# A two-block model kernel on one core: setup by halves of the features, first projections pulled into it, bias rows moved behind the turning of the tokens

## The reference

```python
mod_x = silu(c) @ w_mod + b_mod            # shift | scale | gate, 1024 each; the same for c_ctx
hx = rmsnorm(x, norm_g) * (1 + sc_x) + sh_x          # 512 tokens
hc = rmsnorm(ctx, norm_g) * (1 + sc_c) + sh_c        # 256 tokens
z  = h @ w_in        # aq, ak, av, ag, alr, bq, bk, bv, bg, bbeta, bdec, mg
alog = log_sigmoid(alr @ gla_up + gla_ub) / 16       # decay of the first mixer, both directions
# a gated linear attention over chunks of 64 (aq, ak, av, alog) and a gated delta rule
# (bq, bk, bv), both forward and backward; gated, merged, projected by w_o, gated, added to x
```

## Time and profile before

| | |
|---|---|
| median of 3 runs | 1430.29 us (1427.27 to 1430.88) |
| the profiled execution's own time | 1430.24 us |
| its span, first to last instruction | 1428.1 us |
| TensorE busy | 1360.0 us (95% of the span) |
| VectorE / ScalarE / GpSimd busy | 623.8 / 412.3 / 330.2 us |
| TensorE's share of the chain that ended last | 87% |
| mean granted TensorE clock | 0.987 |

### The profile page before, as it was taken

The page is one execution under the profiler, slowest core; times in us unless marked ns, Lnnn a source line. Parts: engine busy times, 40 slices in busy tenths (PEclk is TensorE's granted clock), DMA queues, the critical chain, the costliest instruction groups (busy, mean ns, idle before and its releaser), DMA issues.

```text
span 1428.1 us, 22760 instructions
## 1 busy us (share of the span) xinstructions
PE 1360.0 (95%) x9123; PEld 775.6 (54%) x9123; DVE 623.8 (44%) x1330; ACT 412.3 (29%) x892; POOL 330.2 (23%) x422
## 2 busy tenths in 40 slices
PE   4999989999999999999999999998899999999897
PEld 2454645555566777764444655445554645445553
DVE  3364264975234333452146321226745330326735
ACT  3332031226332222110002301235732211226631
POOL 0200000112123443210043000025733000016731
PEclk9999989999999999999999999999999999999999
DMA  9611000211230010003241612311000713210001
GB/s 335 213 59 55 5 33 27 74 59 40 79 120 3 3 61 3 3 1 132 104 152 51 159 55 59 148 59 49 1 16 1 185 51 107 81 57 1 2 1 59
DMA packets 71512, 96.48 MB, mean 68 GB/s; under 512 B 27623, under 2 KB 35231, under 8 KB 71406
## 3 DMA queue, kind: packets, MB, share of 16 engines
q1 hardware_dynamic: 71034, 94.76, 19.8%
q10 hardware_dynamic: 372, 0.27, 0.1%
HBM read 92.89 MB, written 2.13 MB: 67 GB/s over the span
## 4 chain that ended last, share of the span: by engine, by line
PE 87%; DVE 7%; ACT 2%; issue 2%; POOL 1%; DMA 1%; ACTq 0%; DVEq 0%; POOLq 0%
PE PS L147 83%; PE PS L2543 2%; DVE AR L2649 1%; ACT AR L2771 1%; DVE AR L2636 1%; DMA AR<-in_onehot 1%; DVE AR L1900 0%; POOL AR L2849 0%; PE PS L347 0%; DVE AR L812 0%; POOL AR L2830 0%; PE PS L1958 0%; ACT AR L2781 0%; DVE AR L773 0%; POOL AR L370 0%
## 5 line engine op out<-in xcount | busy, mean ns | idle before, releaser
L147 PE MATMUL PS<-AR 64*64 64x64 f32 (+13 forms) x8534 | 1291.6, 347 | 28.3 <-ACT AR L2781 6.6
L147 PEld LDWEIGHTS PS<-AR 64*64 64x64 f32 (+4 forms) x8534 | 711.3, 156 | 580.0 <-issue 487.3
L2771 ACT ACTIVATE AR<-AR 128x257 f32<-128x257 f32 (+5 forms) x160 | 84.9, 530 | 104.9 <-DVE AR L2649 96.0
L370 POOL TENSOR_TENSOR AR<-AR 128x1 f32<-128x1 f32 (+4 forms) x26 | 21.9, 840 | 359.9 <-DVE AR L365 313.2
L2649 DVE CUSTOM_DVE_ANT_0 AR<-PS,AR 128x257 f32<-128x257 f32 (+5 forms) x160 | 72.3, 452 | 67.3 <-PE PS L147 49.3
L1107 DVE SCALAR_TENSOR_TENSOR AR<-AR 128x441 f32<-128x441 f32 (+2 forms) x96 | 78.5, 818 | 17.9 <-ACT AR L1064 14.3
L1493 DVE TENSOR_TENSOR AR<-PS,AR 128x256 f32<-128x256 f32 x60 | 25.5, 425 | 114.6 <-PE PS L147 111.5
L2830 POOL TENSOR_SCALAR AR<-AR 128x257 f32<-128x257 f32 (+5 forms) x96 | 53.4, 557 | 62.6 <-DVE AR L2655 55.0
L1847 POOL TENSOR_TENSOR AR<-AR 128x512 f32<-128x512 f32 x36 | 47.5, 1319 | 58.9 <-DMA AR<-in_w_o 55.8
L2543 PE MATMUL PS<-AR 128*128 128x128 f32 x352 | 51.2, 283 | 8.4 <-DVE AR L2636 6.3
L1620 ACT ACTIVATE AR<-PS 128x512 f32<-128x512 f32 x48 | 28.7, 597 | 101.8 <-PE PS L147 99.4
(11 more groups left out here) (253 smaller groups left out, 823.5 us busy)
## 6 DMA issues: line engine op xcount, KB each, us to landing
AR<-in_w_in SPq DMA_DIRECT2D x17, 2048.0 KB, 8.9
AR<-in_w_mod SPq DMA_DIRECT2D x6, 2048.0 KB, 16.4
AR<-in_w_out SPq DMA_DIRECT2D x4, 2048.0 KB, 12.8
AR<-in_x SPq DMA_DIRECT2D x8, 512.0 KB, 5.5
AR<-in_w_o SPq DMA_DIRECT2D x2, 2048.0 KB, 8.5
AR<-in_w_in SPq DMA_DIRECT2D x2, 1664.0 KB, 8.8
AR<-in_w_in SPq DMA_DIRECT2D x12, 256.0 KB, 4.1
AR<-in_w_gla_out SPq DMA_DIRECT2D x1, 2048.0 KB, 8.9
```

The lines of the kernel that those rows point to most:

```text
L147: return t.matmul(o, l, r, start=s, stop=p, skip_group_check=True)
L2771: a_.do.activation(P, P, ACT.Exp, bias=mn[:, j % NJS, e:e + 1], scale=-1.0, accum_out=su[:, j % NJS, e:e + 1]).then_inc(sa, na("p", l, j, e))
```

## The change

1. SP issues `w_mod` parts 0 and 2 (shift and scale of features 0 to 511), load 0 and the first four feature tiles of load 1 (semaphore `s_aq`), then `w_mod` parts 1 and 3 and the last four tiles of load 1. One transfer more than before; the same bytes.
2. TensorE's bias row matmuls stand behind `mod_turned(2)`, VectorE's copies of them behind the modulation of the first half.
3. Modulation goes by halves: k = 0, 2 and tiles 0 to 3 of `hT` and `hC`, then k = 1, 3 and tiles 4 to 7. VectorE's `turned` is split in `row` (copy) and `turned`.
4. Halves of the first projections stand between these steps: `low_rank(t, 0)`, `queries(0, 0, 4)`, `queries(1, 0, 2)`, `queries(1, 2, 4)`. Their second halves and the rest stand in `gla_t`.
5. Several accumulators get named banks, and `ps.ring` is set to seven banks for `u` and `bb`.
6. In `gla_t` the second half of the `aq` 1 projection stands before `key(0)`, where it stood behind it. `gla_v`, `gla_a` and `gla_g` are unchanged.

The diff, cut to what matters (the removed loops are described above):

```diff
@@ setup_s
-        for k in range(4):
-            s.go.dma_start(wmod[:, k], wm(512 * k)[0]).then_inc(s_wm[k], 16)
-        load(s, 0)
-        load(s, 1)
+        aq, = wviews(1)
+        for half, ks in ((0, (0, 2)), (1, (1, 3))):
+            for k in ks:
+                s.go.dma_start(wmod[:, k], wm(512 * k)[0]).then_inc(s_wm[k], 16)
+            if half == 0:
+                load(s, 0)
+            sl = slice(4 * half, 4 * half + 4)
+            s.go.dma_start(aq[:, sl, :], wl[1][0][0][:, sl, :]).then_inc(s_ring[ring_slot(1)] if half else s_aq, 16)
@@ setup_t
-            p = ps.take(t, "mod", k)
+            p = ps.take(t, "mod", k, bank=k // 2 if k % 2 else None)
-            p = ps.take(t, "modT", k)
+            p = ps.take(t, "modT", k, bank=2 + k // 2 if k % 2 else None)
...
+        mod(2)
         mod_turned(0)
-        for k in range(1, 4):
-            mod(k)
-            mod_turned(k)
+        mod_turned(2)
+        t.wait_ge(s_oh, 32)
+        t.wait_ge(sv, nv["rt"])
+        for i, (k, lo, hi) in enumerate(BIAS):
+            p = ps.take(t, "brow", k, lo, bank=i)
+            mm(t.go, p[0:13, 0:hi - lo], rt[0:33, 0:13], oh[0:33, 640 * k + lo:640 * k + hi], True, True).then_inc(st, nt("brow", k, lo))
+        low_rank(t, 0)
+        mod(1)
+        queries(t, 0, 0, 4)
+        mod_turned(1)
+        mod(3)
+        queries(t, 1, 0, 2)
+        mod_turned(3)
+        queries(t, 1, 2, 4)
+    def low_rank(t, half):
...
+            b = 4 if lo else 5
+            p = ps.banks[b] if half else ps.take(t, "alr", lo, bank=b)
+            for i in range(2 * half, 2 * half + 2):
...
+    def queries(t, a, t0, t1):
+        w, = weights(t, 1) if t0 >= 4 else wviews(1)
+        t.wait_ge(s_aq, 16)
+        p = ps.banks[6 + a] if t0 else ps.take(t, "aq", a, bank=6 + a)
+        for t8 in range(t0, t1):
...
+        if t1 == 8:
+            x.then_inc(st, nt("aq", a))
@@ setup_v
+        row(0)
         for m in range(0, 8, 2):
             v.wait_ge(st, nt["hC", m])
...
+        row(2)
+        turned(0)
+        turned(2)
+        modulated(0)
+        for k, lo, hi in BIAS:
+            v.wait_ge(st, nt["brow", k, lo])
...
+        row(1)
+        turned(1)
+        row(3)
+        turned(3)
+        modulated(1)
@@ setup_a
+        for half in range(2):
+            for k in (half, 2 + half):
+                a.wait_ge(sv, nv["modAB", k])
...
@@ gla_t
+        low_rank(t, 1)
+        queries(t, 0, 4, 8)
+        ps.ring = list(range(7))
...
-        query(0)
         t.wait_ge(s_up, 64)
         t.wait_ge(sv, nv["alr", 0])
         for q, lo, hi in UQ:
...
         x.then_inc(st, nt("bb"))
+        queries(t, 1, 4, 8)
+        ps.ring = list(range(8))
         key(0)
-        query(1)
         key(1)
```

More of the change, by code:

```diff
@@ L287, in program @@
     s_wm = [landing(f"w_mod{k}") for k in range(4)]
+    s_aq = landing("gla_queries_first_half")
     s_x = [landing(f"x{i}") for i in range(6)]
@@ L356, in setup_t @@
             x.then_inc(st, nt("hC", m))
+        mod(2)
         mod_turned(0)
-        for k in range(1, 4):
-            mod(k)
-            mod_turned(k)
-        nt.mark("at", "setup")
+        mod_turned(2)
[12 more added lines that the diff above has]
+        queries(t, 1, 2, 4)
+        nt.mark("at", "setup")
+    def low_rank(t, half):
+        w, = weights(t, 0)
+        for lo, hi in XC:
+            hx, h = (hT, "hT") if lo else (hC, "hC")
+            b = 4 if lo else 5
+            p = ps.banks[b] if half else ps.take(t, "alr", lo, bank=b)
+            for i in range(2 * half, 2 * half + 2):
+                for q in range(2):
+                    t8 = 2 * i + q
+                    t.wait_ge(*((sa, na[h, t8]) if t8 % 2 else (sv, nv[h, t8])))
+                    x = mm(t.go, p[64 * q:64 * q + 64, 0:hi - lo], w[:, t8, :], hx[:, t8, :], i == 0, i == 3)
+            if half:
+                x.then_inc(st, nt("alr", lo))
+        if half:
+            nt.mark("weights", 0)
+    def queries(t, a, t0, t1):
[3 more added lines that the diff above has]
+        for t8 in range(t0, t1):
+            t.wait_ge(*((sa, na["hT", t8]) if t8 % 2 else (sv, nv["hT", t8])))
+            x = mm(t.go, p[:, :], w[:, t8, 128 * a:128 * a + 128], hT[:, t8, :], t8 == 0, t8 == 7)
+        if t1 == 8:
+            x.then_inc(st, nt("aq", a))
     def rsq_v(v, o, x, scale, *name):
@@ L387, in setup_v, with row @@
         v.do.scalar_tensor_tensor(out=bg, in0=vc("bmod", 8, 8), scalar=1.0, in1=vc("norm_g", 0, 8), op0=ALU.add, op1=ALU.mult).then_inc(sv, nv())
[L388 to L393, removed]
+        def row(k):
             v.wait_ge(st, nt["mod", k])
@@ L397, in turned @@
             ps.empty(sv, nv, "mod", k)
+        def turned(k):
             c = slice(4 * (k % 2), 4 * (k % 2) + 4)
@@ L408, in turned, with modulated @@
             ps.empty(sv, nv, "modT", k)
+        def modulated(half):
+            for m in range(4 * half, 4 * half + 4, 2):
+                v.do.tensor_scalar(hT[:, m, :], hT[:, m, :], modA[:, m:m + 1], modB[:, m:m + 1], ALU.mult, ALU.add).then_inc(sv, nv("hT", m))
+            for m in range(4 * half, 4 * half + 4, 2):
+                v.do.tensor_scalar(hC[:, m, :], hC[:, m, :], modA[:, 8 + m:9 + m], modB[:, 8 + m:9 + m], ALU.mult, ALU.add).then_inc(sv, nv("hC", m))
         v.wait_ge(sa, na["squares", 5])
@@ L425, in setup_v @@
             ps.empty(sv, nv, "hC", m)
[L426 to L432, removed]
+        row(2)
[4 more added lines that the diff above has]
+            v.wait_ge(st, nt["brow", k, lo])
+            v.do.tensor_copy(brow[0:13, 640 * k + lo:640 * k + hi], ps["brow", k, lo][0:13, 0:hi - lo]).then_inc(sv, nv("brow"))
+            ps.empty(sv, nv, "brow", k, lo)
+        row(1)
[3 more added lines that the diff above has]
+        modulated(1)
         nv.mark("at", "setup")
@@ L455, in setup_a @@
             ps.empty(sa, na, "hC", m)
[L456 to L461, removed]
+        for half in range(2):
+            for k in (half, 2 + half):
+                a.wait_ge(sv, nv["modAB", k])
+            for m in range(4 * half + 1, 4 * half + 4, 2):
+                a.do.activation(hT[:, m, :], hT[:, m, :], ACT.Identity, bias=modB[:, m:m + 1], scale=modA[:, m:m + 1]).then_inc(sa, na("hT", m))
+            for m in range(4 * half + 1, 4 * half + 4, 2):
+                a.do.activation(hC[:, m, :], hC[:, m, :], ACT.Identity, bias=modB[:, 8 + m:9 + m], scale=modA[:, 8 + m:9 + m]).then_inc(sa, na("hC", m))
         na.mark("at", "setup")
@@ L554, in gla_t @@
     def gla_t(t):
[L555 to L565, removed]
+        low_rank(t, 1)
+        queries(t, 0, 4, 8)
+        ps.ring = list(range(7))
         w, = weights(t, 1)
-        def query(a):
-            p = ps.take(t, "aq", a)
-            projT(t, p, w, 128 * a, 128, 256, 768, ("aq", a))
         def key(a):
```

5 lines of the change are left out of this document (removed).

## The result

| | before | after |
|---|---|---|
| median, 4 runs each (lowest to highest) | 1430.05 us (1427.27 to 1430.88) | 1439.57 us (1437.88 to 1444.14) |
| ratio, 95% interval | | 1.0071 (1.005 to 1.0092) |
| profiled execution, its span | 1430.24, 1428.1 us | 1437.88, 1435.7 us |

The change makes the kernel slower by about 0.7%, clear of the 0.3% that a measurement can tell; the forecast was 1440.2 us. The profiled execution after is the fastest of its four, so its trace says +7.6 us where the medians say +9.5.

A forecast was written before the change was run, and what follows sets the result against it. TensorE (87% of the chain) bounds the kernel, but VectorE's chain decides until the second turning. Stall +7.3, cold clock +1.5 and +1.5, banks -0.3 make +10.0 on 1430.24: 1440.2 us, range 1435.5 to 1443.5.

The forecast's parts named there:

- The deciding mechanism: First mixer: key(0) waits 10.5 us for ScalarE's late copy of aq 1; queries and second turning move +7.3 us before clock.
- the count of banks: First mixer's ring: key(0) takes k = 31, bank 7, the bank of aq 1; before, k = 42, bank 2.
- the wait for `key(1)` that goes: VectorE's copies in the first mixer: its 1.61 us wait for key(1) disappears, so +8.9 becomes +7.3 us.
- What the setup gains (c): TensorE's setup steps: aq 0 done about 52.8 instead of 58.3, 5.5 us ahead, plus 3.4 us of aq 1 done.
- That most of the lead can't be spent (d): Before u: TensorE idles 2.8 us for up, held by bias rows landing at 52; u starts 2.5 us earlier.
- the rivals on the landing of the bias rows: Setup transfers: earlier landing gives 1437.3 us (chance 0.05); later setup or transfers give 1442 to 1444 us (0.10).
- the rule on the order of completions: Transfer queues: completions are not first in, first out per issuing engine, so bias row stores may land earlier: -2.9 us.
- The sum: Whole kernel: +7.3 + 1.5 + 1.5 - 0.3 = +10.0 us on 1430.24, so 1440.2 us.
- 1.5 of clock: key(0) starts cold after 10.5 us of idle TensorE, making VectorE's sums 1.5 us later.
- the gap of about 3 us ending at 55.7: Sign in TensorE's timeline: idle for about 3 us before u, ended at 55.7 by the transfer of up.
- the one on the other side (no stall): First mixer: key(0) gets a bank other than 7, the gain stands, 1426 to 1428 us; chance 0.05.
- The one in which the change doesn't do what it says: Setup: turning doesn't start earlier, the 5.6 us lead is gone, u starts near 58: +2.5, 1442.7 us.

The follow-up runs named there:

- experiment 1: Changed kernel with the ring kept at seven banks until key(1) is issued, so key(0) avoids the bank of aq 1: 1427.18 us, ratio 0.9991.
- experiment 3: Kernel before, with only query(1) put ahead of key(0) and key(0) taking the bank of aq 1: 1446.51 us, ratio 1.0111.
- experiment 6: Changed kernel, seam fixed (ring cut, key(0) first), up loaded during setup, u behind alr, second aq halves behind key(0), aq copies after the logarithm: 1427.7 us, ratio 0.9975.
- experiment 2: Changed kernel with the ring at seven banks until key(1) and key(0) back ahead of the second half of aq 1: 1426.2 us, ratio 0.9981.
- experiment 5: Changed kernel with seven-bank ring and key(0) ahead of aq 1's second half, bias rows moved back ahead of the turning: 1431.84 us, ratio 1.0007.
- second trace of before: The kernel before, unedited, executed once more for a second trace: 1431.47 us.
- experiment 4: Changed kernel plus eleven unread matmuls of 512 columns in a free bank between aq 1 and key(0), filling TensorE's wait: 1443.52 us, ratio 1.0087.

## Why the prediction was right, and which of its terms were off

**The deciding mechanism** was right in each step: the count of banks (`key(0)` gets the bank of `aq` 1), ScalarE's list as the releaser, VectorE's list as what turns the wait of TensorE into late sums, the wait for `key(1)` that goes, and VectorE's chain as the one that decides until the second turning. Experiments 1 and 3 show it from both sides: taken out, the loss is gone; put into the old kernel, it is there, though together with the new order, which by the estimate there has 5.9 of the 14.5 us at the sums.

**What the setup gains (c)** was wrong. Turning (17.36, forecast 17.5) and `mod(0)` (23.12, forecast 22.8) were on time, but TensorE ended `aq` 0 at 58.1, forecast 52.8. Of these 5.3 us, 3.4 are 6.8 us at half clock in the middle of the setup, which nothing in the trace before showed: the same steps with waits between them kept 1.00 there. Some 1 us is a longer turning (5.83 for 5.25) and steps sized too short, and the last 0.8 a wait of the weight loads for a modulated tile ahead of the second half of `alr`. I had let TensorE's steps follow each other at full clock without bounding that.

**That most of the lead can't be spent (d)** came out true for another reason. The forecast had TensorE wait 2.8 us for `up`, released by the bias rows' landing, and `u` 2.5 us early. In fact POOL was released by ScalarE's last modulated tile (L511) at 53.36 and not by the stores. Its timeline and SP's, after:

```profile
53.36 0.53 POOL L955 MEMSET AR<- 128x512 f32 x1 [35.09 <-ACT AR L511]
```

```profile
53.92 1.71 SPq L597 DMA_DIRECT2D AR<-in_gla_up  x4
```

TensorE was no earlier than before, and it didn't wait; ScalarE's chain started at 64.78, 0.17 us early in place of 2.5. The stores had landed by 53.36, so no more than 1.4 us later than before; how much earlier, no row tells. So the rivals on the landing of the bias rows had no say: a store that lands earlier would have changed nothing, and the rule on the order of completions that stood beside them was not tried by any run.

**The sum** then reads: sums late by 14.4 (forecast 8.9 and 1.5 of clock): 8.9 as forecast, 2.3 for the setup's missing lead, 2.9 for the clock in place of 1.5 (`key(0)` took 77.81 to 91.10, 13.3 us for 10.4), and 0.3 that these round off. Less 1.6 for the wait at `key(1)`, as forecast: 12.9 at the second turning, forecast 8.8. There TensorE was idle for 2.86 and 1.32 us and ran cold as forecast (0.50 from 117.4 on, 1.54 us for a turning of 0.88); another 2.5 us came until the first mixer's end, forecast 1.2. That makes 15.4, forecast 10.0. The same stretch, from the second turning to the first mark, costs experiment 1 3.5 us without the wait, and experiment 6 0.3; the first has 27.3 us at half clock between 100 and 400 us, as the changed kernel has, the second 17.0, as the kernel before has. So this part seems to be clock too, and the idle pieces ahead of the turnings (2.85 and 1.91 us in experiment 1, one of 1.34 in experiment 6) its likely cause; no run separates them.

**The clock behind the first mixer** gave 7.2 us of this back in one trace and 3.9 in the other. This term wasn't in the sum at all. So the total, 9.5 us between medians against a forecast of 10.0, is right in sign and in its cause and partly lucky in its size: the stall was priced 4.1 us too low at the second turning and 5.4 at the first mark, and the give-back was left out. Of the signs that it named, the gap of about 3 us ending at 55.7 didn't come, and the sums and the second turning came later than it had them (91.65 for 86 to 88, 120.89 for 116 to 117).

**The rivals**: the one on the other side (no stall) did not come; experiment 1 is what it describes, and measured 1427.18 where it had 1426 to 1428, though by another sum, since the setup's lead was missing. The one in which the change doesn't do what it says is half true: turning starts early, and `u` doesn't, but its reason (turning at its old time) fell.

## What to carry to other kernels

When accumulators come from a ring, a step moved ahead of another moves every later take: count the takes up to the first one that lands on a bank whose emptying stands far down another engine's list, because in-order lists turn a copy of 0.6 us into a wait of 10. When a step is pulled ahead to fill gaps, ask what stands in the list between it and the chain that decides; here half a projection ahead of `key(0)` was enough to use up the gain (queries at 92.91 in experiment 1, at 90.64 in experiment 2). And price a wait of TensorE by the late release of what follows, plus the cold clock after it, and not by its own length.

## What the runs showed of the hardware

- TensorE's granted clock fell to 0.50 (1.2 GHz) in the setup of the changed kernel and of every variant of it (beginning between 31 and 39 us, for 3.4 or 6.8 us), in all but one of them with TensorE's instructions back to back (in experiment 5 an idle 1.14 us stood just ahead), where the kernels with the old setup show 1.00 through the setup in all three traces. (The column shows 1.00 at the cold start too, where half as many turnings ran as three microseconds later, so it says nothing of the first turnings.) What TensorE had done just before: the modulation's matmuls of 32 columns, turnings of two columns and, but for experiment 5, the bias rows. As the clock fell in experiment 5 too, the bias rows aren't needed for it; which of the others it is, or whether it is the missing waits, was not tried.
- After 9.83 us of idle TensorE the clock was at 0.50 from inside the wait until 5.4 us after it, and cost `key(0)` 2.9 us. The Trainium skill, "TensorE: Matmul & The Clock Gate", Terms, prices this at half the throttled time; for 5.4 us of work under it that is an estimate of 2.7, so the trace agrees within 0.2.
- Executions of one kernel differ by stretches of about 3.4 us at half clock in dense parts of the second half of the first block, 1.7 us each (none and two in the two traces of the changed kernel, 255.7 and 259.0 us between the marks). Elsewhere such a stretch can cost nothing (6.8 us near 980 in the second trace of before). So kernels that differ by 3 us at the edit can end in either order: experiment 4 has its sums 2.9 us ahead of the changed kernel, and a span 6.4 us longer (1442.1, 1435.7).
